# Key weights between the index chunks, one low part on GpSimd, a later angle table and a folded scale in the first stage of a two-block transformer kernel

## What is computed

```python
proj = x @ w_in
q, k, v, iq, ik, iw = jnp.split(proj, A_SPLITS, axis=-1)   # 1024, 256, 256, 8*64, 64, 8 columns
q, k, iq, ik = partial_rotary(each, cos, sin)
iw = iw.astype(jnp.float32) * IDX_HEADS ** -0.5
s = jnp.einsum('bqhd,bsd->bqhs', iq_b, ik) * IDX_DIM ** -0.5
score = jnp.einsum('bqh,bqhs->bqs', iw_b, jax.nn.relu(s))
_, sel = lax.top_k(where(causal, score, -inf), 64)
```

## Time and profile before

| | before |
|---|---|
| median of three executions | 1236.24 us |
| the profiled execution, its own time | 1236.22 us |
| its span | 1234.5 us |
| TensorE, busy time and share | 1222.5 us, 99% |
| VectorE | 846.8 us, 69% |
| ScalarE | 588.7 us, 48% |
| GpSimd | 95.0 us, 8% |
| granted TensorE clock | 1.00 in every slice |

### The profile page before, as it was taken

The page is one execution under the profiler, slowest core; times in us unless marked ns, Lnnn a source line. Parts: engine busy times, 40 slices in busy tenths (PEclk is TensorE's granted clock), DMA queues, the critical chain, the costliest instruction groups (busy, mean ns, idle before and its releaser), DMA issues.

```text
span 1234.5 us, 18696 instructions
## 1 busy us (share of the span) xinstructions
PE 1222.5 (99%) x7924; PEld 1043.6 (85%) x7924; DVE 846.8 (69%) x1000; ACT 588.7 (48%) x714; POOL 95.0 (8%) x222
## 2 busy tenths in 40 slices
PE   8999999999999999999999999999999999999998
PEld 7888888888888888888988888888898888888887
DVE  6886766665866776666766676667587666666675
ACT  6774434444744544333654444435462544444434
POOL 4541000001000200000101000001000100000000
PEclk9999999999999999999999999999999999999999
DMA  9425655556534755554616655655654357555642
GB/s 337 150 71 182 226 176 200 187 189 171 191 138 136 242 202 183 193 196 137 239 44 203 206 191 185 201 176 204 197 192 144 103 158 239 191 194 181 205 140 99
DMA packets 126819, 222.08 MB, mean 180 GB/s; under 512 B 6000, under 2 KB 90496, under 8 KB 126736
## 3 DMA queue, kind: packets, MB, share of 16 engines
q1 hardware_dynamic: 123840, 210.88, 50.9%
q0 software_dynamic: 2896, 10.01, 2.6%
HBM read 219.82 MB, written 1.05 MB: 179 GB/s over the span
## 4 chain that ended last, share of the span: by engine, by line
PE 92%; DMA 2%; DVE 2%; ACT 2%; issue 1%; POOL 1%; SPq 0%
PE ps L794 20%; PE ps L622 17%; PE ps L796 11%; PE ps L599 10%; PE ps L600 10%; PE ps L601 10%; PE ps L762 4%; PE ps L706 2%; PE ps L806 2%; DVE wlo L1830 1%; DMA raw<-in_mlp_w_up 1%; DMA raw<-in_ffn_w_in 1%; PE ps L970 1%; ACT whi L1381 1%; DMA raw<-in_a_w_in 1%
## 5 line engine op out<-in xcount | busy, mean ns | idle before, releaser
L1830 DVE TENSOR_TENSOR wlo<-raw,whi 128x2048 fp32r<-128x2048 f32 (+3 forms) x204 | 452.6, 2232 | 175.3 <-ACT whi L1381 173.8
L1381 ACT ACTIVATE whi<-raw 128x2048 fp32r<-128x2048 f32 (+3 forms) x204 | 377.0, 1861 | 76.0 <-DMA raw<-in_hgrn_w_in 21.2
L794 PE MATMUL ps<-xhl,whi 128*128 128x512 f32 x1088 | 271.5, 391 | 0.0
L794 PEld LDWEIGHTS ps<-xhl,whi 128*128 128x128 f32 x1088 | 198.5, 188 | 37.5
L622 PE MATMUL ps<-whi,xhl 128*128 128x512 f32 (+2 forms) x736 | 183.9, 382 | 0.9 <-DVE wlo L1830 0.5
L599 PE MATMUL ps<-whi,hh 128*128 128x512 f32 x432 | 168.9, 391 | 0.0
L600 PE MATMUL ps<-whi,hl 128*128 128x512 f32 x432 | 168.6, 390 | 0.0
L601 PE MATMUL ps<-wlo,hh 128*128 128x512 f32 x432 | 168.1, 389 | 0.0
L796 PEld LDWEIGHTS ps<-xhl,wlo 128*128 128x128 f32 x1088 | 148.4, 190 | 10.6
L622 PEld LDWEIGHTS ps<-whi,xhl 128*128 128x128 f32 x736 | 131.6, 188 | 26.6 <-DVE wlo L1830 1.2
L796 PE MATMUL ps<-xhl,wlo 128*128 128x256 f32 x1088 | 151.7, 282 | 0.0
(11 more groups left out here) (329 smaller groups left out, 1335.3 us busy)
## 6 DMA issues: line engine op xcount, KB each, us to landing
raw<-in_ffn_w_in SPq DMA_DIRECT2D x40, 1024.0 KB, 5.1
raw<-in_mlp_w_up SPq DMA_DIRECT2D x32, 1024.0 KB, 5.4
raw<-in_mlp_w_down SPq DMA_DIRECT2D x32, 1024.0 KB, 4.9
raw<-in_ffn_w_down SPq DMA_DIRECT2D x22, 1024.0 KB, 4.8
raw<-in_hgrn_w_in SPq DMA_DIRECT2D x16, 1024.0 KB, 5.5
raw<-in_b_w_in SPq DMA_DIRECT2D x12, 1024.0 KB, 5.1
raw<-in_ple_w_gate SPq DMA_DIRECT2D x8, 1024.0 KB, 5.9
raw<-in_a_w_in SPq DMA_DIRECT2D x5, 1024.0 KB, 6.8
```

The lines of the kernel that those rows point to most:

```text
L794: mm(bank(b + f), w[0][:, kk, P * f : P * f + P], xhl[:, kk, :, :].rearrange("p a n -> p (a n)"), start=(kk == 0), stop=False)
L1381: a.activation(whi[:, slot, 0:w], raw[:, slot, 0:w], ACT.Copy).then_inc(s["hi_done"], 1)
L1830: v.tensor_tensor(wlo[:, slot, 0:w], raw[:, slot, 0:w], whi[:, slot, 0:w].bitcast(F32), ALU.subtract).then_inc(s["lo_done"], 1)
```

## The change

- The key chunks become three, of 2, 2 and 4 slabs, as chunks 2, 6 and 7: one after the second index chunk, two behind the last. All later chunks move up by one number. PE treats them as the index chunks (`first_rows`), without a wait for xT.
- `dsa_v`'s low part is made by POOL, behind the second causal mask of the score and ahead of the rotation of q; PE waits for `beside_lo` there.
- Table 1: `angles(1)` on DVE stands behind the low part of `dsa_q` chunk 0 and the copy of the keys, its sines behind the high part of `dsa_q` chunk 2, `tables(1)` behind the low part of `dsa_q` chunk 3.
- The scale of the index weights (L493) is left out and folded into the factor of the ReLU.

```diff
@@ -160,10 +160,15 @@
...
         IQ_PARTS = [(0, 1), (1, 1), (2, 2), (4, 2), (6, 2)]
-        for k0, kn in IQ_PARTS:
-            chunk("dsa_iq", rows_of(a_in, k0, kn, A_IQ, 512), kn, 512)
-        for k0 in (0, 4):
-            chunk("dsa_keys", rows_of(t["key_columns"], k0, 4, 0, A_KEYS), 4, A_KEYS)
+        KEY_PARTS = [(0, 2), (2, 2), (4, 4)]
+        IQ_AT, KEY_AT = [0, 1, 3, 4, 5], [2, 6, 7]
+        for n in range(len(IQ_AT) + len(KEY_AT)):
+            if n in IQ_AT:
+                k0, kn = IQ_PARTS[IQ_AT.index(n)]
+                chunk("dsa_iq", rows_of(a_in, k0, kn, A_IQ, 512), kn, 512)
+            else:
+                k0, kn = KEY_PARTS[KEY_AT.index(n)]
+                chunk("dsa_keys", rows_of(t["key_columns"], k0, kn, 0, A_KEYS), kn, A_KEYS)
         square_chunks("dsa_q", a_in, A_Q)
@@ -225,6 +230,7 @@
...
         N_CHUNKS = len(width)
+        BESIDE = first["dsa_v"]
@@ -246,9 +252,10 @@
...
             for n in range(N_CHUNKS):
-                if n < len(IQ_PARTS):
-                    k0, kn = IQ_PARTS[n]
-                    sp.dma_start(xT[:, k0 : k0 + kn, :], t["x_columns"][:, k0 : k0 + kn, :]).then_inc(s[f"xT_landed{n}"], 16)
+                if n in IQ_AT:
+                    q = IQ_AT.index(n)
+                    k0, kn = IQ_PARTS[q]
+                    sp.dma_start(xT[:, k0 : k0 + kn, :], t["x_columns"][:, k0 : k0 + kn, :]).then_inc(s[f"xT_landed{q}"], 16)
                 if n == first["dsa_q"] + 3:
@@ -489,8 +496,7 @@
...
                 last = g.tensor_copy(ikdup[:, tt, :, :], ikw[:, tt, 0:A_HD].unsqueeze(1).broadcast_to([P, 2, A_HD]))
-            step(last)
-            g.tensor_scalar(ikw[:, :, A_HD:A_SMALL], ikw[:, :, A_HD:A_SMALL], float(IDX_HEADS**-0.5), None, ALU.mult).then_inc(s["index_rotated"], 1)
+            last.then_inc(s["index_rotated"], 1)
             pool.wait_ge(s["k_act"], 1)
@@ -502,6 +508,9 @@
...
                                 base=b * P, pattern=[[-1, P * (b + 1)]], channel_multiplier=1).then_inc(s["score_masked"], 1)
+            pool.wait_ge(s["hi_done"], BESIDE + 1)
+            slot, w = BESIDE % RING, width[BESIDE]
+            g.tensor_tensor(wlo[:, slot, 0:w], raw[:, slot, 0:w], whi[:, slot, 0:w].bitcast(F32), ALU.subtract).then_inc(s["beside_lo"], 1)
             for b in range(TT):
@@ -606,7 +615,10 @@
...
-                pe.wait_ge(s["lo_done"], n + 1)
+                if n == BESIDE:
+                    pe.wait_ge(s["beside_lo"], 1)
+                else:
+                    pe.wait_ge(s["lo_done"], n + 1)
@@ -1007,28 +1019,28 @@
             pe.wait_ge(s["ident_done"], 1)
-            def index_queries(q):
-
-                k0, kn = IQ_PARTS[q]
-                n = first["dsa_iq"] + q
-                w = weights(n, kn, 512)
+            def first_rows(n, k0, kn, cols, b0, wait_x):
+
+                w = weights(n, kn, cols)
                 for part, w_part in ((0, 0), (1, 0), (0, 1)):
...
                     else:
-                        pe.wait_ge(s["xT_lo" if part else "xT_hi"], q + 1)
+                        wait_x(part)
                         pe.wait_ge(s["hi_done"], n + 1)
...
                         for tt in range(TT):
-                            last = mm(bank(2 + tt), (xh, xl)[part][:, k0 + kk, P * tt : P * tt + P], w[w_part][:, kk, :],
+                            last = mm(bank(b0 + tt, cols), (xh, xl)[part][:, k0 + kk, P * tt : P * tt + P], w[w_part][:, kk, :],
                                       start=(k0 + kk == 0 and (part, w_part) == (0, 0)), stop=(k0 + kk == KD - 1 and w_part == 1))
...
             keep_fed(14)
-            for q in range(len(IQ_PARTS)):
-                index_queries(q)
-            for i in range(2):
-                by_rows(first["dsa_keys"] + i, 4, A_KEYS, 4 * i, KD, [(tt, slice(0, A_KEYS), bank(4 + tt, A_KEYS)) for tt in range(TT)])
+            for n in range(len(IQ_AT) + len(KEY_AT)):
+                if n in IQ_AT:
+                    q = IQ_AT.index(n)
+                    first_rows(n, *IQ_PARTS[q], 512, 2, lambda part: pe.wait_ge(s["xT_lo" if part else "xT_hi"], q + 1))
+                else:
+                    first_rows(n, *KEY_PARTS[KEY_AT.index(n)], A_KEYS, 4, lambda part: None)
@@ -1582,24 +1594,32 @@
...
-            for q, (k0, kn) in enumerate(IQ_PARTS):
-                act.wait_ge(s[f"xT_landed{q}"], 16)
-                a.activation(xh[:, k0 : k0 + kn, :], xT[:, k0 : k0 + kn, :], ACT.Copy).then_inc(s["xT_hi"], 1)
-                until(first["dsa_iq"] + q)
-            until(first["dsa_keys"])
-            for w, (sn, cs) in enumerate(((sinA, cosA), (sinM, cosM))):
+            for n in range(IQ_AT[-1] + 1):
+                if n in IQ_AT:
+                    q = IQ_AT.index(n)
+                    k0, kn = IQ_PARTS[q]
+                    act.wait_ge(s[f"xT_landed{q}"], 16)
+                    a.activation(xh[:, k0 : k0 + kn, :], xT[:, k0 : k0 + kn, :], ACT.Copy).then_inc(s["xT_hi"], 1)
+                until(n)
+
+            def sines(w, sn, cs):
+
                 act.wait_ge(s["angle_done"], w + 1)
...
                 a.activation(cs[:, :, :], cs[:, :, :], ACT.Sin, scale=0.5).then_inc(s["sines_done"], 1)
-                until(first["dsa_keys"] + 1)
-            act.wait_ge(s["w_done"], first["dsa_iq"] + len(IQ_PARTS))
+
+            until(KEY_AT[1])
+            sines(0, sinA, cosA)
+            until(KEY_AT[2])
+            act.wait_ge(s["w_done"], IQ_AT[-1] + 1)
             a.activation(kvi[:, 0, 512:1024], bank(2), ACT.Copy).then_inc(s["iq_act"], 1)
             until(first["dsa_q"])
-            act.wait_ge(s["w_done"], first["dsa_keys"] + 2)
+            act.wait_ge(s["w_done"], KEY_AT[-1] + 1)
             for tt in range(TT):
...
             a.activation(kvi[:, 0, 0:FG], ps[:, 4, A_SMALL:A_KEYS], ACT.Copy).then_inc(s["k_act"], 1)
-            until(first["dsa_q"] + 1)
+            until(first["dsa_q"] + 2)
+            sines(1, sinM, cosM)
             until(first["dsa_q"] + 3)
@@ -1611,7 +1631,7 @@
...
                     act.wait_ge(s["index_added"], u - 3)
-                a.activation(relu_s[:, u % 4, :], bank(4 + u % 4), ACT.Relu, scale=float(A_HD**-0.5)).then_inc(s["index_relu"], 1)
+                a.activation(relu_s[:, u % 4, :], bank(4 + u % 4), ACT.Relu, scale=float(A_HD**-0.5 * IDX_HEADS**-0.5)).then_inc(s["index_relu"], 1)
             until(first["dsa_o"] + 1)
@@ -1825,9 +1845,12 @@
...
             def lo_part(n):
+                if n == BESIDE:
+                    return
                 slot, w = n % RING, width[n]
                 dve.wait_ge(s["hi_done"], n + 1)
-                v.tensor_tensor(wlo[:, slot, 0:w], raw[:, slot, 0:w], whi[:, slot, 0:w].bitcast(F32), ALU.subtract).then_inc(s["lo_done"], 1)
+                v.tensor_tensor(wlo[:, slot, 0:w], raw[:, slot, 0:w], whi[:, slot, 0:w].bitcast(F32), ALU.subtract).then_inc(
+                    s["lo_done"], 2 if n == BESIDE + 1 else 1)
@@ -2125,10 +2148,13 @@
...
-            for q, (k0, kn) in enumerate(IQ_PARTS):
-                dve.wait_ge(s["xT_hi"], q + 1)
-                v.tensor_tensor(xl[:, k0 : k0 + kn, :], xT[:, k0 : k0 + kn, :], xh[:, k0 : k0 + kn, :].bitcast(F32), ALU.subtract).then_inc(s["xT_lo"], 1)
-                until(first["dsa_iq"] + q)
+            for n in range(IQ_AT[-1] + 1):
+                if n in IQ_AT:
+                    q = IQ_AT.index(n)
+                    k0, kn = IQ_PARTS[q]
+                    dve.wait_ge(s["xT_hi"], q + 1)
+                    v.tensor_tensor(xl[:, k0 : k0 + kn, :], xT[:, k0 : k0 + kn, :], xh[:, k0 : k0 + kn, :].bitcast(F32), ALU.subtract).then_inc(s["xT_lo"], 1)
+                until(n)
@@ -2152,18 +2178,16 @@
...
             angles(0, sinA, cosA, 0, ROT)
-            until(first["dsa_keys"])
+            until(KEY_AT[1])
             tables(0, cosA)
+            dve.wait_ge(s["w_done"], IQ_AT[-1] + 1)
+            v.tensor_copy(kvi[:, 1, 512:1024], bank(3)).then_inc(s["iq_dve"], 1)
+            until(first["dsa_q"])
+            dve.wait_ge(s["small_out"], TT)
+            v.tensor_copy(kvi[:, 1, 0:FG], ps[:, 5, A_SMALL:A_KEYS]).then_inc(s["k_dve"], 1)
             angles(1, sinM, cosM, ROT, M_HALF)
-            dve.wait_ge(s["w_done"], first["dsa_iq"] + len(IQ_PARTS))
-            v.tensor_copy(kvi[:, 1, 512:1024], bank(3)).then_inc(s["iq_dve"], 1)
-            until(first["dsa_keys"] + 1)
+            until(first["dsa_q"] + 3)
             tables(1, cosM)
-
-            until(first["dsa_q"] + 1)
-            dve.wait_ge(s["w_done"], first["dsa_keys"] + 2)
-            v.tensor_copy(kvi[:, 1, 0:FG], ps[:, 5, A_SMALL:A_KEYS]).then_inc(s["k_dve"], 1)
-            until(first["dsa_v"])
             dve.wait_ge(s["index_rotated"], 1)```

On PE, at the key chunks. The names: `whi` and `wlo` are the high and low part of a weight, `xhl` both parts of the turned x, `ps` the accumulators. Before, behind the last index chunk:

```order
L622 MATMUL ps<-whi,xhl 128x328 [waits lo_done]
L622 MATMUL ps<-whi,xhl 128x328 x7
```

## The result

| | before | after |
|---|---|---|
| median, runs side by side | 1236.70 us (22 executions) | 1238.41 us (22 executions) |
| ratio | | 1.0014, 95% interval 1.0008 to 1.0020 |
| the profiled execution | 1236.22 us | 1238.78 us |
| its span | 1234.5 us | 1237.0 us |

The interval excludes no change, and the median lies 1.7 us on the wrong side: the forecast was 1234.6, its range ended at 1237.2.

A forecast was written before the change was run, and what follows sets the result against it. TensorE bounds the kernel (92% of the chain of waits), its start bound by loading, then the keys' low parts. Starting dsa_q 1.6 us earlier gave 1236.24 - 1.6 = 1234.6 us, range 1233.6 to 1237.2.

The forecast's parts named there:

- the sentence on the angle instructions: Before VectorE's next long subtraction: ten angle instructions beside GpSimd each stretch 0.1 us, so it starts at 28.6, after GpSimd's copies.
- my two undisturbed times: Race at the index-key copies: VectorE's next long subtraction can start at 27.65 if undisturbed; GpSimd reaches its copies at 28.05.
- The rival of the caught copies: GpSimd's two index-key copies each wait for a VectorE subtraction; TensorE turns at 32.7, 0.3 us late: 1236.6 us; chance 0.17.
- more than the copies caught: An index-key rotation instruction on GpSimd is held too; signal at 35.0, 2.7 us over before: 1238.9 us; chance 0.10.
- The key chunk on the queue: DMA queue: the early 336 KB key chunk delays everything behind it by 0.95 us; third index chunk starts at 11.35.
- the third rival: The key chunk costs the DMA queue more: third index chunk at 12.0 or later, gain 0.5 to 1.1, 1235.4 us; chance 0.12.
- the keys end without a stop: TensorE's other 36 key matmuls run without waiting and end at 25.0, 1.9 us earlier than before.
- the wait for the low part of `dsa_q`: TensorE, free at 25.0, waits for VectorE's low part of chunk 0 (25.1 to 25.4); dsa_q starts at 25.3, gain 1.6 us.
- GpSimd's subtraction: The value chunk's low part, moved to GpSimd, takes 4.7 us within 7.25 us of idle time ahead of 54.29.
- the fold: Leaving out GpSimd's index-weight scale saves 2.25 us there; worth nothing alone, it matters because TensorE now arrives at 30.8.

The follow-up runs named there:

- The wait: The changed kernel with VectorE waiting for index_rotated between angles(1) and the low part of dsa_q chunk 1: 1235.76 us beside 1236.71, ratio 0.9991.
- the three copies: The changed kernel with three useless VectorE copies out of PSUM ahead of the angle instructions: 1235.46 us beside 1236.52, ratio 0.9992.
- the table early: The changed kernel with the second angle table (angles, sines, tables) back in its old place: 1243.12 us, ratio 1.0050.
- the key parts alone: The kernel before with only the split into three key chunks and their pass order: 1241.90 us, ratio 1.0042.
- the pass order alone: The kernel before with its two four-slab key chunks, still behind the index chunks, multiplied high/high first: 1241.96 us, ratio 1.0037.
- the keys last: The changed kernel with the keys as two four-slab chunks behind all index chunks, in the new pass order: 1235.55 us beside 1236.48, ratio 0.9993.

## Why the prediction was wrong

- **The step that failed** is the sentence on the angle instructions: "If ten stretch by only 0.1 each, VectorE starts at 28.6 and GpSimd is through." It gave 1.0 us of stretch to VectorE and none to GpSimd. The angle instructions are eight and not ten (two, one, one, three and one in the order of the change). Only the first two stretched, 0.62 us against 0.38 in the earlier trace rows, by 0.24 in all. And GpSimd's small rotations beside them, for which the prediction had no stretch, took as much longer: from the first of them to the copies it is 28.82 - 27.25 = 1.57 us in the change, against 29.11 - 27.81 = 1.30 before.

```profile
27.81 0.23 POOL L478 TENSOR_TENSOR rot<-ikw,cosA 128x16 f32<-128x16 f32 x1
```

  So the stretching bought GpSimd nothing, and what decided were my two undisturbed times, 27.65 and 28.05, by which VectorE led by 0.40 us. VectorE came 0.94 us later than its time: 0.66 since TensorE ended the keys later than forecast, 0.24 stretched. GpSimd came 0.77 later: 0.5 since its first instruction was held until 22.91 and not 22.4, and 0.26 stretched. That leaves 0.23, as in the trace. That VectorE did start at 28.59, as my sentence has it, is chance. The numbers that spoke for the loss stood in the text; one row of 0.48 us, stretched over ten instructions, outweighed them. The wait and the three copies show that this step alone turns a gain of about 1.0 us into a loss of 1.7.
- **The rival of the caught copies** happened, and its price was too low. It had TensorE turn at 32.7; it turned at 33.41, for the subtractions started 0.94 us later than the 27.65 used there. And no case had the clock, 1.62 us in the profiled execution, about 0.7 by the ratios. The measured 1238.4 lies near the 1238.9 of the rival *more than the copies caught*, but by luck: VectorE was over 0.2 us early, and still no rotation was caught, since the last one had started at 28.53. That rival's mechanism is seen in the kernels with the table early, with the key parts alone and with the pass order alone, at 4.6 to 6.2 us.
- **The key chunk on the queue**: 0.95 us was too little on the mean. From the high part of the second index chunk to that of the third, ScalarE's timeline has 10.79 - 7.00 = 3.79 us in the change; over the ten profiles with the early key chunk that distance is 3.35 to 4.53, 4.07 on the mean, and in the three with the keys last and the third chunk whole 2.38 to 3.02, 2.68 on the mean. That is about 1.4 us. The third index chunk came at 11.99, not 11.35: the third rival, all but reached. In this one profile, though, the queue accounts for only half of the delay. Before the change ScalarE's rows are

```profile
6.18 0.63 ACT L1381 ACTIVATE whi<-raw 128x512 fp32r<-128x512 f32 x1 [1.10 <-DMA raw<-in_a_w_in]
```

  and, with the third index chunk, 9.20; with the change they are

```profile
7.00 0.63 ACT L1393 ACTIVATE whi<-raw 128x512 fp32r<-128x512 f32 x1 [1.90 <-DMA raw<-in_a_w_in]
...
10.79 1.06 ACT L1393 ACTIVATE whi<-raw 128x1024 fp32r<-128x1024 f32 x1 [1.37 <-DMA raw<-in_a_w_in]
```

  Of the 1.59 us by which the third index chunk came later, 0.82 were there with the second one, ahead of the key chunk, and 0.77 came behind it. So the 0.66 us by which the keys ended later than forecast are a late landing more than a price of the key chunk.
- **Right, with other sizes**: the keys end without a stop, at 25.66 instead of 25.0; the wait for the low part of `dsa_q` did not come, as TensorE was later than it. The gain at the turn, without the race, would be 1.24 us, and with the race won (the wait, the three copies) 1.0 to 1.1 were measured, not 1.6.
- **Right**: GpSimd's subtraction takes 4.62 us (4.7 estimated) and is hidden: the rotation of q still waits 3.21 us for ScalarE behind it. VectorE's top 64 is not slowed by it:

```profile
50.01 0.62 DVE L2211 MAX8 top<-work 128x8 f32<-128x128 f32 x2
```

  the same 0.62 us as in the earlier trace rows, in the middle of GpSimd's 48.43 to 53.05. The Trainium skill (Perfetto Trace Analysis, section Optimizing Scalar/DVE Operations) cautions that work moved between these two engines might not help, since they share a read port. I had priced that at up to 4.7 us; beside MAX8, whose row has one input, the trace shows none of it.
- **Not shown**: that the fold matters once TensorE comes early. With the scale back the ratio is 1.0014 as in the change, but there GpSimd is late for another reason; no run has the scale back where the race is won.
